# Second mixer's end: later spreads, layer norm's bias on VectorE, one root behind the tanh

## The chip, the cores and the metric

The kernel runs on one core of one Trainium2 chip, in one launch. Its time is the device time of an execution in microseconds, the median of several runs. Engines: TensorE (PE: matmuls; PEld: its weight loads), VectorE (DVE), ScalarE (ACT), GpSimd (POOL), SyncE (SP, here only DMA issues). Each engine runs its own queue in order; semaphores tie them together.

## The reference, cut to what matters

Two transformer blocks on 512 tokens of width 1024, in float32: attention beside a state space mixer and a feed-forward layer, then a block whose mixer has two halves. The change touches only the end of this second mixer:

```python
y_conv = conformer_conv(u_a, u_b, ...)          # 4 chunks of 128 channels
y_ret = retention_group(hq, hk, hv, hg)         # 4 heads of 128 channels
y = concatenate([y_conv, y_ret]) @ w_out

def conformer_conv(u_a, u_b, dw_w, dw_b, ln_w, ln_b):
    y = conv(u_a * sigmoid(u_b), dw_w) + dw_b   # depthwise, 31 taps
    return silu(layernorm(y, ln_w, ln_b))       # over 512 channels

def retention_group(hq, hk, hv, hg):
    q, k = rotary(hq), rotary(hk)               # per head
    o = chunkwise_retention(q, k, hv)
    o = o * rsqrt(mean(o * o) + EPS)            # per head and token
    return silu(hg) * o
```

## The kernel before

Everything lies with channels on the 128 partitions and the 512 tokens along the free axis. A matrix product in float32 is made of three reduced-precision matmuls (`exact`, L497 to L499): high weights by high input, high by low, low by high. So each weight unit (128 output channels by 1024 input channels, 8 tiles) is split by ScalarE into its high half (`split`, L1123) and by GpSimd into its low half, in a ring of four slots; and each input chunk must be there as a high half (a copy on ScalarE) and a low half (a subtraction on VectorE).

The second mixer first makes its inputs by units: a and b for the convolution, then q2, k2, v2, g2 for each of four heads (`unit2`, 24 matmuls each). Beside them VectorE works off the list of convolution taps (`taps`, L2628), each of which reads the accumulator that the previous tap of its channel chunk wrote. For each head: the rotation of query and key (`rotate`, and for the last head `rotated_last`, L2644), the scores (`ret_scores`, L946), `decayed`, the values (`ret_values`, L964), the square on ScalarE (`ret_square`, L1714), its column sums on TensorE (`ret_sum`, L972), the root on ScalarE (`row_root`, L1719), the reciprocal root on VectorE (`ret_var` L2669, `row_factor` L2673 to L2679), its spread over all partitions on TensorE (`spread`, L980), and `ret_norm` on VectorE (L2688, L2690), whose result ScalarE copies (`ret_high`, L1723). Sqrt and Tanh are in different tables of ScalarE: `load_root_table` is a tiny Sqrt that brings the first one in (L1160).

The convolution ends with `conv_out` on ScalarE (L1678), the mean over channels on TensorE (`conv_mean`, L990), `centre` on VectorE (L2698), squares on ScalarE (L1771), their sums (`conv_squares`, L1000), the root, the factor and a spread as above. Then for each of four chunks: `ln_scale` (VectorE, L2703), `ln_tanh` (ScalarE: a tanh, L1781, and an affine copy, L1783), `conv_silu` (VectorE, L2708), `conv_high` (ScalarE, L1787) and `conv_rest` (VectorE, L2713), which releases the chunk to TensorE.

TensorE's first three outputs of out2 are made chunk by chunk of the input (`out2_chunk`, 9 matmuls each), in the order of `OUT2_CHUNKS` = (4, 5, 6, 0, 1, 2, 3, 7): heads one to three, the four convolution chunks, the fourth head. Among these calls stand the last steps of the fourth head. The other outputs follow without a wait for inputs. The order on each engine is written out by hand, and it alone decides what waits for what.

Of the kernel before, what the change touches and what calls it, by code (L numbers as in the profile page):

```python
# [9 lines left out]
ALU = mybir.AluOpType  # L10
# [167 lines left out]
def block_program(nc, weights, x, p, vectors, constants, att_tables, ret_tables, acs_dram, out):  # L178
# [3 lines left out]
    def place(name, shape, dt=F32, at=None):  # L182

        size = 4 * int(np.prod(shape[1:]))
        offset = top[0] if at is None else at
        if at is None:
            top[0] += (size + 31) // 32 * 32
        return nc.alloc_sbuf_tensor_at(name, shape, dt, offset=offset)
# [81 lines left out]
    r_v = place("r_v", [P, T], at=r_at + 4 * K)  # L270
    r_g = place("r_g", [P, 2, T], at=r_at + 6 * K)
    ln_t = place("ln_t", [P, 4, T], at=work)
    rot_q = place("rot_q", [P, T], at=t_at)
    rot_k = place("rot_k", [P, T], at=t_at + 2 * K)
    rot_s = place("rot_s", [P, 2, T], at=t_at + 4 * K)
# [39 lines left out]
    def sem(name):  # L315
        if name not in sems:
            sems[name] = nc.alloc_semaphore(name)
        return sems[name]
# [44 lines left out]
    with block:  # L363
# [126 lines left out]
        def _(pe):  # L490
# [437 lines left out]
            def unit2(name, between={}, apart=0, bank=None):  # L928

                job = JOBS[name]  # L930
                pe.wait_ge(lo_done, job.unit + 1)
                pe.wait_ge(out_free[job.bank], job.m + 1 - apart)
                for t in range(TILES):
                    if t in between:
                        between[t]()
                    last = exact(ps[job.bank if bank is None else bank][:], job.unit % RING, t, u_hi[:, t, :], u_lo[:, t, :],
                                 t == 0, t == TILES - 1, job.unit)
                last.then_inc(out_ready[job.bank], 1)
# [44 lines left out]
            def ret_spread(h):  # L983
                spread(6, ROW["ret", h]).then_inc(sem("ret_rb"), 1)

            def conv_mean(c0, c1):

                for c in range(c0, c1):
                    pe.wait_ge(sem("conv_done"), max(c + 1, 3))
                    last = mm(ps[2][:], ones, cv[:, c, :], start=(c == 0), stop=(c == 3))  # L990
                if c1 == 4:
                    last.then_inc(sem("mean_sum"), 1)
# [12 lines left out]
            def out2_chunk(n):  # L1005

                c = OUT2_CHUNKS[n]
                if c >= 4:
                    pe.wait_ge(sem("ret_split"), c - 3)
                else:  # L1010
                    pe.wait_ge(sem("conv_split"), c + 1)
                for j in range(3):
                    job = JOBS["out2", j]
                    if n == 0:
                        pe.wait_ge(lo_done, job.unit + 1)
                        if job.bank < 2:
                            pe.wait_ge(out_free[job.bank], job.m + 1)
                        else:
                            pe.wait_ge(sem("conv_done"), 4)
                    last = exact(ps[job.bank][:], job.unit % RING, c, v_hi[:, c, :], v_lo[:, c, :], n == 0, n == C8 - 1)  # L1020
                    if n == C8 - 1:
                        last.then_inc(out_ready[job.bank], 1)
# [7 lines left out]
            for h in range(R_HEADS):  # L1030
# [9 lines left out]
                    ret_sum(h - 1)  # L1040
                if h < last_head:
                    unit2(("g2", h))
            unit2(("g2", last_head), {3: lambda: ret_spread(last_head - 1), 5: lambda: conv_mean(0, 3)})
            conv_mean(3, 4)
            ret_scores(last_head)
            values_turn(last_head)
# [4 lines left out]
            spread(2, ROW["ln"]).then_inc(sem("ln_rb"), 1)  # L1051
            ret_sum(last_head)
            out2_chunk(1)
            out2_chunk(2)
            ret_spread(last_head)
            for n in range(3, C8):
                out2_chunk(n)
            for c in range(3, WHOLE):
                job = JOBS["out2", c]
                pe.wait_ge(lo_done, job.unit + 1)  # L1060
                if job.bank < 2:
                    pe.wait_ge(out_free[job.bank], job.m + 1)
                for t in range(TILES):
                    last = exact(ps[job.bank][:], job.unit % RING, t, v_hi[:, t, :], v_lo[:, t, :], t == 0, t == TILES - 1)
                last.then_inc(out_ready[job.bank], 1)
# [48 lines left out]
        def _(act):  # L1114
# [593 lines left out]
            def ret_square(h):  # L1708
                act.wait_ge(sem("retained"), h + 1)
                if h:  # L1710
                    act.wait_ge(sem("ret_summed"), h)
                else:
                    act.wait_ge(sq_used, STATS["pre2"][0])
                af(sq[:, 0, :], ps[7][:], ACT.Square).then_inc(sem("ret_squared"), 1)  # L1714

            def row_root(n):
                act.wait_ge(sem("row_var"), n + 1)
                var, sd, _ = ROW_AT[n]
                af(tiny[:, sd:sd + QB], tiny[:, var:var + QB], ACT.Sqrt).then_inc(sem("row_sd"), 1)  # L1719

            def ret_high(h):
                act.wait_ge(sem("ret_normed"), h + 1)
                af(v_hi[:, h + 4, :], r_o[:], ACT.Copy).then_inc(sem("ret_hi"), 1)  # L1723
# [49 lines left out]
            gate_tanh(last_head)  # L1773
            load_root_table()
            row_root(ROW["ln"])
            ret_square(last_head)
            row_root(ROW["ret", last_head])

            def ln_tanh(c):
                act.wait_ge(sem("ln_scaled"), c + 1)  # L1780
                af(ln_t[:, c, :], cv[:, c, :], ACT.Tanh, scale=0.5, bias=half[:, c:c + 1]).then_inc(sem("ln_tanh"), 1)  # L1781
                act.wait_ge(sem("ln_tanh"), c + 1)
                af(cv[:, c, :], cv[:, c, :], ACT.Identity, scale=0.5, bias=half[:, c:c + 1]).then_inc(sem("ln_biased"), 1)  # L1783

            def conv_high(c):
                act.wait_ge(sem("conv_silu"), c + 1)
# [2 lines left out]
            ln_tanh(0)  # L1789
            ln_tanh(1)  # L1790
            conv_high(0)
            ret_high(last_head)
            ln_tanh(2)
            conv_high(1)
            ln_tanh(3)
            conv_high(2)
            conv_high(3)

            q, _ = STATS["post2"]
            for c in range(WHOLE):  # L1800
# [136 lines left out]
        def _(dve):  # L1937
# [763 lines left out]
            def ln_scale(c):  # L2701
                dve.wait_ge(sem("ln_rb"), 1)
                stt(out=cv[:, c, :], in0=cv[:, c, :], scalar=v("ln_w", c), in1=ps[2][:], op0=ALU.mult, op1=ALU.mult)\  # L2703
                    .then_inc(sem("ln_scaled"), 1)

            def conv_silu(c):
                dve.wait_ge(sem("ln_biased"), c + 1)
                stt(out=cv[:, c, :], in0=ln_t[:, c, :], scalar=1.0, in1=cv[:, c, :], op0=ALU.add, op1=ALU.mult)\  # L2708
                    .then_inc(sem("conv_silu"), 1)

            def conv_rest(c):
# [39 lines left out]
            ret_var(2)  # L2751
            taps(115, 117)
            row_factor(ROW["ret", 2])
            taps(117, 119)
            ret_norm(2)
            taps(119, len(CONV_TAPS))
            rotate(3)
            rotated_last()
            for c in range(4):
# [5 lines left out]
            row_var(ROW["ln"], ps[2][:, 0:QB], D_CONV)  # L2765
            row_factor(ROW["ln"])
            ln_scale(0)
            ln_scale(1)
            ret_var(3)
            ln_scale(2)  # L2770
            ln_scale(3)
            row_factor(ROW["ret", 3])
            conv_silu(0)
            ret_norm(3)
            conv_rest(0)
            conv_silu(1)
            conv_rest(1)
            ret_rest(3)
            conv_silu(2)
            conv_rest(2)  # L2780
            conv_silu(3)
            conv_rest(3)


            halved_norm("post2", y_u, "fpre2", 40)
# [291 lines left out]
```

## Time and profile before

| what | us |
| --- | --- |
| median of 3 runs | 1786.79 |
| lowest and highest of them | 1786.18 to 1786.8 |
| the profiled execution's own time | 1786.4 |
| its span in the trace | 1784.6 |
| TensorE busy | 1753.3 |
| VectorE busy | 842.1 |
| ScalarE busy | 767.9 |
| GpSimd busy | 783.8 |

The span is what the trace covers; the execution's own time has 1.8 us around it. Busy times of the engines overlap. TensorE's granted clock was full in this stretch. The end of a matmul is modelled, so matmuls that follow each other directly overlap in the rows. Times inside the trace are counted from the span's start.

### The profile page before, as it was taken

The numbers are of one execution on the slowest core, as the hardware profiler recorded it, in microseconds if no ns is written. First come the engines' busy times: TensorE is split into PE (matmuls) and PEld (weight loads), VectorE is DVE, ScalarE is ACT, GpSimd is POOL, SyncE is SP. The second block draws the span as 40 slices with busy tenths as digits, with TensorE's granted clock in tenths as the row PEclk, the third lists the DMA queues.
The fourth block names the chain that finished last, engine by engine and source line by source line (L and its number), as shares of the span: only waits on it lengthen the run. The fifth ranks groups of instructions, "written<-read, shape, count | busy, mean of one in ns | idle before, by whom it ended". The sixth has DMA issues, their size and how long they took to land.

```text
span 1784.6 us, 24772 instructions
## 1 busy us (share of the span) xinstructions
PE 1753.3 (98%) x8990; PEld 1452.4 (81%) x8990; DVE 842.1 (47%) x1587; ACT 767.9 (43%) x1269; POOL 783.8 (44%) x603
## 2 busy tenths in 40 slices
PE   7999999999999999999999999999999999999998
PEld 5777788888888888888888888988779888888877
DVE  7654546677777311263111113799847433320044
ACT  6444654566664322443222234445565323222253
POOL 3322344433343555515444446265442544445543
PEclk9999999999999999999999999999999999999998
DMA  5222233332323223314222323132221332233321
GB/s 200 72 63 81 72 108 112 112 107 95 107 95 130 95 94 96 117 49 153 94 96 94 96 95 116 61 106 71 71 79 52 107 100 99 94 95 106 106 83 48
DMA packets 47950, 170.70 MB, mean 96 GB/s; under 512 B 5457, under 2 KB 7633, under 8 KB 47601
## 3 DMA queue, kind: packets, MB, share of 16 engines
q1 hardware_dynamic: 44496, 156.25, 26.9%
q10 hardware_dynamic: 3360, 13.17, 2.2%
q8 instruction: 62, 1.02, 0.2%
q14 instruction: 32, 0.25, 0.0%
HBM read 167.24 MB, written 2.16 MB: 95 GB/s over the span
## 4 chain that ended last, share of the span: by engine, by line
PE 95%; DVE 3%; ACT 1%; issue 0%; DMA 0%; DVEq 0%; POOLq 0%; POOL 0%; SPq 0%; ACTq 0%
PE bank L497 29%; PE bank L499 28%; PE bank L498 28%; DVE bank L2628 1%; PE bank L707 1%; PE bank L855 1%; PE bank L716 1%; PE bank L729 1%; PE bank L859 1%; PE bank L839 1%; PE bank L535 1%; PE bank L830 0%; PE bank L964 0%; PE bank L946 0%; PE bank L613 0%
## 5 line engine op out<-in xcount | busy, mean ns | idle before, releaser
L411 POOL TENSOR_TENSOR w_lo<-raw,w_hi 128x512 fp32r<-128x512 f32 x472 | 619.3, 1334 | 783.9 <-ACT w_hi L1123 783.9
L497 PE MATMUL bank<-u_hi,w_hi 128*128 128x512 f32 (+1 forms) x1456 | 567.3, 390 | 3.6 <-DVE tmp L2547 3.4
L499 PE MATMUL bank<-u_hi,w_lo 128*128 128x512 f32 (+1 forms) x1456 | 557.9, 383 | 0.0
L498 PE MATMUL bank<-u_lo,w_hi 128*128 128x512 f32 (+1 forms) x1456 | 557.1, 383 | 0.0
L1123 ACT ACTIVATE w_hi<-raw 128x1024 fp32r<-128x1024 f32 x279 | 293.3, 1052 | 264.8 <-PE bank L499 262.0
L497 PEld LDWEIGHTS bank<-u_hi,w_hi 128*128 128x128 f32 x1456 | 274.1, 188 | 58.1 <-issue 7.0
L499 PEld LDWEIGHTS bank<-u_hi,w_lo 128*128 128x128 f32 x1456 | 274.0, 188 | 54.7
L498 PEld LDWEIGHTS bank<-u_lo,w_hi 128*128 128x128 f32 x1456 | 274.4, 188 | 51.3 <-issue 0.2
L419 POOL TENSOR_TENSOR w_lo<-raw,w_hi 128x512 fp32r<-128x512 f32 x84 | 111.0, 1344 | 185.7 <-ACT w_hi L1123 185.7
L497 PE MATMUL bank<-v_hi,w_hi 128*128 128x512 f32 (+1 forms) x368 | 133.8, 364 | 2.8 <-DVE v_lo L2713 2.8
L498 PE MATMUL bank<-v_lo,w_hi 128*128 128x512 f32 (+1 forms) x368 | 133.0, 361 | 0.0
L499 PE MATMUL bank<-v_hi,w_lo 128*128 128x512 f32 (+1 forms) x368 | 133.0, 361 | 0.0
L2628 DVE SCALAR_TENSOR_TENSOR bank<-cat,vec,bank 128x512 f32<-128x512 f32 x120 | 83.5, 751 | 4.3 <-ACT bank L1674 3.4
L2268 DVE SCALAR_TENSOR_TENSOR post<-bank,vec,post 128x511 f32<-128x511 f32 (+2 forms) x96 | 71.8, 748 | 27.1 <-ACT post L1304 22.0
L2547 DVE SCALAR_TENSOR_TENSOR tmp<-bank,tmp 128x512 f32<-128x512 f32 x32 | 22.1, 692 | 125.3 <-ACT tmp L1599 125.3
L497 PEld LDWEIGHTS bank<-v_hi,w_hi 128*128 128x128 f32 x368 | 69.4, 189 | 14.4 <-DVE v_lo L2713 3.8
L2559 DVE TENSOR_TENSOR ffn_acc<-ffn_acc,bank 128x512 f32<-128x512 f32 x29 | 19.9, 687 | 127.3 <-PE bank L499 127.3
L499 PEld LDWEIGHTS bank<-v_hi,w_lo 128*128 128x128 f32 x368 | 69.4, 189 | 10.7
L498 PEld LDWEIGHTS bank<-v_lo,w_hi 128*128 128x128 f32 x368 | 69.5, 189 | 10.6
L1952 DVE TENSOR_TENSOR diag<-diag,sq 128x512 f32<-128x512 f32 x24 | 21.9, 913 | 105.9 <-ACT sq L1143 105.8
L497 PE MATMUL bank<-h_hi,w_hi 128*128 128x512 f32 x176 | 68.5, 389 | 0.0
L498 PE MATMUL bank<-h_lo,w_hi 128*128 128x512 f32 x176 | 68.5, 389 | 0.0
(369 smaller groups left out, 2562.1 us busy)
## 6 DMA issues: line engine op xcount, KB each, us to landing
raw<-weights SPq DMA_DIRECT2D x289, 512.0 KB, 3.6
bc<-acs ACTq DMA_DIRECT2D x16, 512.0 KB, 3.9
xs<-x SPq DMA_DIRECT2D x4, 512.0 KB, 7.4
xs<-x ACTq DMA_DIRECT2D x1, 2048.0 KB, 7.9
rt<-ret_tables ACTq DMA_DIRECT2D x1, 1536.0 KB, 6.5
out<-xs SPq DMA_DIRECT2D x12, 128.0 KB, 1.8
dist<-att_tables SPq DMA_DIRECT2D x1, 512.0 KB, 3.3
p_raw<-p ACTq DMA_DIRECT2D x1, 512.0 KB, 7.3
```

What stands on the lines that cost most here:

```text
L411: return nc.gpsimd.tensor_tensor(w_lo[:, slot, w], raw[:, slot, w], w_hi[:, slot, w].bitcast(F32), ALU.subtract)
L419: last = nc.gpsimd.tensor_tensor(lo[:, w], raw[:, u % RING, w], hi[:, w].bitcast(F32), ALU.subtract)
L497: mm(dst, high[:, w], hi, start=first, stop=False)
L498: mm(dst, high[:, w], lo, start=False, stop=False)
L499: return mm(dst, low[:, w], hi, start=False, stop=last)
L535: last = mm(ms[:, 2 * h + t:2 * h + t + 1], part[:, t * P:(t + 1) * P], ones[:, 0:1], start=(n == 0), stop=(n == len(parts) - 1))
L1123: af(halves(u, slot)[0], raw[:, slot, :], ACT.Copy).then_inc(hi_done, 1)
L1952: tt(diag[:], diag[:], sq[:, c % 2, :], ALU.add).then_inc(sq_used, 1)
L2268: last = stt(out=post[:, now, back:T], in0=ps[job.bank][:, 0:T - back], scalar=vec[:, tap:tap + 1], in1=post[:, now, back:T], op0=ALU.mult ...
L2547: stt(out=tmp[:, j % 2, :], in0=ps[bank][:], scalar=0.0, in1=tmp[:, j % 2, :], op0=ALU.max, op1=ALU.mult).then_inc(out_free[j % 2], 1)
L2559: tt(ffn_acc[:, j, :], ffn_acc[:, j, :], ps[j % 2][:], ALU.add).then_inc(out_free[j % 2], 1)
L2628: stt(out=ps[2 + c % 2][:], in0=cat31[:, c, t:t + T], scalar=vec[:, at:at + 1], in1=ps[2 + c % 2][:], op0=ALU.mult, op1=ALU.add).then_inc( ...
```

## The change

On TensorE, `ret_spread` of the third head moves from ahead of tile 3 of the last g2 unit to ahead of tile 6, and the mean of the first three convolution chunks from tile 5 to tile 7. `ret_spread` of the fourth head moves from behind out2_chunk(2) to behind out2_chunk(5). On ScalarE, a tiny Tanh behind the layer norm's root brings the tanh table in ahead of the last square; the affine copy of `ln_tanh` goes; the last head's root moves behind the fourth tanh, with a load of the root table ahead of it and ahead of conv_high(2); `ret_high` of the last head moves to the end. On VectorE, the affine copy comes back as `ln_bias`, into a new tile `ln_b`, with a drain ahead of it and one ahead of each `conv_silu`; the last tap goes ahead of the third head's norm; and the steps of the four chunks are interleaved anew, with row_factor, conv_silu(3), ret_norm(3), conv_rest(3) and ret_rest(3) last, in this order. Nothing else is computed, and no DMA changes.

```diff
--- before.py
+++ after.py
@@ -270,6 +270,7 @@
     r_v = place("r_v", [P, T], at=r_at + 4 * K)
     r_g = place("r_g", [P, 2, T], at=r_at + 6 * K)
     ln_t = place("ln_t", [P, 4, T], at=work)
+    ln_b = place("ln_b", [P, 4, T], at=work + 17 * K)
     rot_q = place("rot_q", [P, T], at=t_at)
     rot_k = place("rot_k", [P, T], at=t_at + 2 * K)
     rot_s = place("rot_s", [P, 2, T], at=t_at + 4 * K)
@@ -1040,7 +1041,7 @@
                     ret_sum(h - 1)
                 if h < last_head:
                     unit2(("g2", h))
-            unit2(("g2", last_head), {3: lambda: ret_spread(last_head - 1), 5: lambda: conv_mean(0, 3)})
+            unit2(("g2", last_head), {6: lambda: ret_spread(last_head - 1), 7: lambda: conv_mean(0, 3)})
             conv_mean(3, 4)
             ret_scores(last_head)
             values_turn(last_head)
@@ -1051,10 +1052,11 @@
             spread(2, ROW["ln"]).then_inc(sem("ln_rb"), 1)
             ret_sum(last_head)
             out2_chunk(1)
-            out2_chunk(2)
-            ret_spread(last_head)
-            for n in range(3, C8):
+            for n in range(2, C8 - 1):
                 out2_chunk(n)
+                if n == 5:
+                    ret_spread(last_head)
+            out2_chunk(C8 - 1)
             for c in range(3, WHOLE):
                 job = JOBS["out2", c]
                 pe.wait_ge(lo_done, job.unit + 1)
@@ -1773,14 +1775,12 @@
             gate_tanh(last_head)
             load_root_table()
             row_root(ROW["ln"])
+            af(tiny[:, 60:61], tiny[:, 63:64], ACT.Tanh)
             ret_square(last_head)
-            row_root(ROW["ret", last_head])
 
             def ln_tanh(c):
                 act.wait_ge(sem("ln_scaled"), c + 1)
                 af(ln_t[:, c, :], cv[:, c, :], ACT.Tanh, scale=0.5, bias=half[:, c:c + 1]).then_inc(sem("ln_tanh"), 1)
-                act.wait_ge(sem("ln_tanh"), c + 1)
-                af(cv[:, c, :], cv[:, c, :], ACT.Identity, scale=0.5, bias=half[:, c:c + 1]).then_inc(sem("ln_biased"), 1)
 
             def conv_high(c):
                 act.wait_ge(sem("conv_silu"), c + 1)
@@ -1789,12 +1789,14 @@
             ln_tanh(0)
             ln_tanh(1)
             conv_high(0)
-            ret_high(last_head)
             ln_tanh(2)
             conv_high(1)
             ln_tanh(3)
+            load_root_table()
             conv_high(2)
+            row_root(ROW["ret", last_head])
             conv_high(3)
+            ret_high(last_head)
 
             q, _ = STATS["post2"]
             for c in range(WHOLE):
@@ -2703,9 +2705,14 @@
                 stt(out=cv[:, c, :], in0=cv[:, c, :], scalar=v("ln_w", c), in1=ps[2][:], op0=ALU.mult, op1=ALU.mult)\
                     .then_inc(sem("ln_scaled"), 1)
 
+            def ln_bias(c):
+                dve.drain()
+                ts(ln_b[:, c, :], cv[:, c, :], 0.5, half[:, c:c + 1], ALU.mult, ALU.add)
+
             def conv_silu(c):
-                dve.wait_ge(sem("ln_biased"), c + 1)
-                stt(out=cv[:, c, :], in0=ln_t[:, c, :], scalar=1.0, in1=cv[:, c, :], op0=ALU.add, op1=ALU.mult)\
+                dve.wait_ge(sem("ln_tanh"), c + 1)
+                dve.drain()
+                stt(out=cv[:, c, :], in0=ln_t[:, c, :], scalar=1.0, in1=ln_b[:, c, :], op0=ALU.add, op1=ALU.mult)\
                     .then_inc(sem("conv_silu"), 1)
 
             def conv_rest(c):
@@ -2751,9 +2758,8 @@
             ret_var(2)
             taps(115, 117)
             row_factor(ROW["ret", 2])
-            taps(117, 119)
+            taps(117, len(CONV_TAPS))
             ret_norm(2)
-            taps(119, len(CONV_TAPS))
             rotate(3)
             rotated_last()
             for c in range(4):
@@ -2765,21 +2771,25 @@
             row_var(ROW["ln"], ps[2][:, 0:QB], D_CONV)
             row_factor(ROW["ln"])
             ln_scale(0)
+            ln_bias(0)
             ln_scale(1)
+            conv_silu(0)
+            ln_bias(1)
             ret_var(3)
             ln_scale(2)
-            ln_scale(3)
-            row_factor(ROW["ret", 3])
-            conv_silu(0)
-            ret_norm(3)
             conv_rest(0)
             conv_silu(1)
+            ln_bias(2)
+            ln_scale(3)
             conv_rest(1)
+            conv_silu(2)
+            ln_bias(3)
+            conv_rest(2)
+            row_factor(ROW["ret", 3])
+            conv_silu(3)
+            ret_norm(3)
+            conv_rest(3)
             ret_rest(3)
-            conv_silu(2)
-            conv_rest(2)
-            conv_silu(3)
-            conv_rest(3)
 
 
             halved_norm("post2", y_u, "fpre2", 40)
```

## Rows read from the trace of the kernel before

**Rows 1.** The page: span, and section 1 (busy us, share of span, instructions).
```profile
span 1784.6 us, 24772 instructions
...
PE 1753.3 (98%) x8990; PEld 1452.4 (81%) x8990; DVE 842.1 (47%) x1587; ACT 767.9 (43%) x1269; POOL 783.8 (44%) x603
```

**Rows 2.** TensorE's waits from 1270 to 1345 us: us in total, times, longest us.
```profile
PE bank L497 <- DVE v_lo L2713: 2.8, 3, 2.1
PE bank L980 <- DVE tiny L2679: 1.8, 1, 1.8
PE bank L972 <- ACT sq L1714: 0.2, 1, 0.2
```

**Rows 3.** Timeline, TensorE, g2, mean, scores: start us, us, line, [idle before <-releaser].
```profile
1276.24 0.39 PE L499 MATMUL bank<-u_hi,w_lo 128*128 128x512 f32 x1
1278.42 0.65 PE L980 MATMUL bank<-cst,tiny 128*128 128x128 f32 x4 [1.79 <-DVE tiny L2679]
...
1284.94 1.02 PE L990 MATMUL bank<-cv,cst 128*128 128x512 f32 x2
1285.80 2.32 PE L946 MATMUL bank<-rot_q,rot_k 128*128 128x512 f32 x8
```

**Rows 4.** Timeline, VectorE, the same stretch.
```profile
1278.28 1.54 DVE L2628 SCALAR_TENSOR_TENSOR bank<-cat,vec,bank 128x512 f32<-128x512 f32 x2
...
1283.67 0.68 DVE L2644 TENSOR_TENSOR rot_k<-rot_k,rot_s 128x512 f32<-128x512 f32 x1
1285.99 2.49 DVE L2698 SCALAR_TENSOR_TENSOR cv<-bank,cv 128x512 f32<-128x512 f32 x4 [1.64 <-PE bank L990]
```

**Rows 5.** Timeline, ScalarE, the same stretch: ret_high(2), then conv_out(3).
```profile
1281.21 0.63 ACT L1723 ACTIVATE v_hi<-r_o 128x512 fp32r<-128x512 f32 x1 [4.33 <-DVE r_o L2690]
1281.88 0.69 ACT L1678 ACTIVATE cv<-bank,vec 128x512 f32<-128x512 f32 x1
```

**Rows 6.** Timeline, TensorE, from the last spread to the last chunk.
```profile
1302.37 0.60 PE L980 MATMUL bank<-cst,tiny 128*128 128x128 f32 x4
1305.12 0.50 PE L497 MATMUL bank<-v_hi,w_hi 128*128 128x512 f32 x1 [2.15 <-DVE v_lo L2713]
...
1310.39 0.50 PE L497 MATMUL bank<-v_hi,w_hi 128*128 128x512 f32 x1 [0.26 <-DVE v_lo L2713]
...
1312.58 0.39 PE L497 MATMUL bank<-v_hi,w_hi 128*128 128x512 f32 x1
...
1314.65 0.39 PE L497 MATMUL bank<-v_hi,w_hi 128*128 128x512 f32 x1
```

**Rows 7.** Timeline, VectorE: ln_scale, row_factor's ends, ret_norm.
```profile
1297.06 1.41 DVE L2703 SCALAR_TENSOR_TENSOR cv<-cv,vec,bank 128x512 f32<-128x512 f32 x2 [1.37 <-PE bank L980]
...
1299.76 0.17 DVE L2673 RECIPROCAL tiny<-tiny 128x4 f32<-128x4 f32 x1
...
1300.50 0.17 DVE L2679 SCALAR_TENSOR_TENSOR tiny<-tiny 128x4 f32<-128x4 f32 x1
...
1303.01 0.69 DVE L2688 SCALAR_TENSOR_TENSOR r_g<-r_g,bank 128x512 f32<-128x512 f32 x1 [0.71 <-PE bank L980]
1303.77 0.69 DVE L2690 TENSOR_TENSOR r_o<-r_g,bank 128x512 f32<-128x512 f32 x1
```

**Rows 8.** Timeline, ScalarE: the last square, the load, the first tanh.
```profile
1296.62 0.60 ACT L1714 ACTIVATE sq<-bank 128x512 f32<-128x512 f32 x1 [1.86 <-PE bank L964]
...
1298.79 1.28 ACT L1781 ACT_TABLE_LOAD   x1
1300.09 0.72 ACT L1781 ACTIVATE ln_t<-cv,half 128x512 f32<-128x512 f32 x1
```

**Rows 9.** Tensor-by-scalar L2186: source view (min/median/max ns), then one of the timeline.
```profile
L2186 DVE TENSOR_SCALAR logits<-logits,tiny x48: 286/420/1525, 37.1 to 203.6; 128x128 f32<-128x128 f32 x12, 128x256 f32<-128x256 f32 x12, 128x384 f32<-128x384 f32 x12, 128x512 f32<-128x512 f32 x12
...
202.93 0.49 DVE L2186 TENSOR_SCALAR logits<-logits,tiny 128x512 f32<-128x512 f32 x1
```

**Rows 10.** Timeline, GpSimd, up to the first weights behind the stretch.
```profile
1316.72 11.44 POOL L419 TENSOR_TENSOR w_lo<-raw,w_hi 128x512 fp32r<-128x512 f32 x8 [27.94 <-ACT w_hi L1123]
```

## The prediction

> **What bounds the kernel now.** First the page's busy times: TensorE is busy 98% of the span [rows 1]. So an edit of the other engines can only win back gaps of TensorE, and the change adds and removes no matmul. Next the waits of TensorE in the stretch from 1270 to 1345 us, the end of the second mixer [rows 2]. They are all that the change can remove there: 1.8 us behind the third head's factor, 0.2 us behind a square and 2.8 us in three waits for the low half of a convolution chunk (v_lo, L2713). That is 4.8 us of 1786.8, or 0.27%. To it comes a little for each restart: the printed idle time runs from the modelled end of a matmul, 0.39 us after its start, though an unbroken follower starts 0.23 us after it (the nine matmuls of a chunk take 2.07 us, 1312.58 to 1314.65, and after a wait 2.19 us, 1310.39 to 1312.58) [rows 3, 6]. So one full wait costs its idle time plus 0.16 + 0.12 = 0.28 us.
>
> Last the three timelines side by side, TensorE, VectorE and ScalarE, for the two places where it stands still. Those are worked through now; times are trace times of the profiled execution, whose span is 1784.6 us [rows 1], while its own time was 1786.4 us and the median of three runs is 1786.79 us. Everything behind the stretch is released by TensorE, or by an engine that waits for TensorE, so I carry a shift of the last out2 matmul to the end in full.
>
> **Part one: the third head's spread, later.** Before, TensorE computes three tiles of g2, then stands 1.79 us until 1278.42 for the factor that VectorE ends at about 1278.4 [rows 3]. After, it has six tiles first: 9 more matmuls by 0.23 us from 1276.47, which is 1278.5. The factor is there, the wait is gone with 0.1 us to spare, and all that follows could start 1.95 us earlier (2.18 us from the last matmul to the spread less the usual 0.23). The scores, at 1285.80 before, would start at 1283.85.
>
> What is late next: the scores need the rotated query and key, and those are VectorE's. VectorE has no idle time from 1278.28 to 1284.35 (0.68 us from 1283.67) [rows 4]. The edit only swaps the last tap of the convolution ahead of the norm of head three. It makes that tap wait for its predecessor (two chained taps take 1.54 us, 0.77 each, where an operation that waits for nothing holds VectorE 0.60, four in 2.49 [rows 4]), so I put the rotated sums 0.1 us later, at about 1284.45. The scores then start at 1284.5, not at 1283.85: 1.3 us earlier, less 0.1 for the restart. On the way, conv_out(3) on ScalarE stands behind ret_high(2), which waits for the norm. Before, it ended at 1281.88 + 0.69 = 1282.57 [rows 5]; now the norm ends 0.75 later, at about 1281.95, then 0.63 and 0.69 us less their overlap give 1283.2. TensorE wants it at 1284.94 - 1.95 = 1283.0 [rows 3], so there is a wait of 0.3 us, but it lies ahead of the one for the rotation and costs nothing of its own. The centring (1.64 us idle before it [rows 4]) can move up by about 1.6 us, more than TensorE. So everything up to ret_values, the spread of ln and ln_scale moves by **1.2 us**; bounds 1.0 (both waits cost a restart) and 1.6 (VectorE as quick as before and the means no obstacle).
>
> **Part two: the end, counted from ln_scale(0)'s start, S** (1297.06 before [rows 7], about 1295.9 after). In front of S, the tanh table: ScalarE is idle 1.86 us in front of the last square [rows 8]. A load takes 1.28 us and its tiny activation some 0.2, 1.5 in all, so it is hidden with 0.35 us to spare. If it weren't, the square and the sum would be late by the excess, one for one. ret_sum's own 0.25 us wait stays.
>
> Durations on VectorE: 0.69 to 0.70 us for a 512-column operation on two tensors (0.60 to the next start when nothing is awaited), and 0.76 from start to start over a drain (1303.01 to 1303.77 [rows 7]). The new ln_bias is a 128x512 tensor-by-scalar operation between two SBUF tiles. The nearest row is one of 0.49 us; the same line goes up to 1.53 us elsewhere, though its median is 0.42 [rows 9]. Here GpSimd is idle 27.94 us up to 1316.72 [rows 10], so I take 0.49; 0.69, the duration of the two-tensor forms, is the bound within this stretch, 1.53 the far one.
>
> The new VectorE order then runs: ln_scale(0) to S+0.7, bias 1.26, ln_scale(1) 1.9, silu(0) 2.65, bias 3.2, ln_scale(2) 3.9, rest(0) 4.55, silu(1) 5.3, bias 5.9, ln_scale(3) 6.5, rest(1) 7.15, silu(2) 7.9. ScalarE fits between: tanh 0.72, copy 0.63 [rows 5, 8], each begun 0.04 us after its input. TensorE has no spread in its way now and wants chunk 0 at S+5.31 (1302.37 before [rows 6]), chunk 1 at 7.37 and chunk 2 at 9.43. The first two are ready at 4.6 and 7.2: both waits go.
>
> Chunk 2 isn't. ScalarE ends the last tanh at 7.25, loads the root table and runs its tiny activation to 8.65, and only then copies: 9.28. rest(2) ends at 10.0, chunk 2 starts at 10.07 and ends at 12.26. The root (0.2 us beside this) and VectorE's row factor (0.91 us, 1299.76 to 1300.67 [rows 7]) are done at 10.85, so the spread starts at 12.26 with no wait.
>
> **Then the old long wait returns at a new place.** On VectorE conv_rest(3) stands behind ret_norm(3), which waits for this spread. Before, conv_rest(0) stood there. From the spread's start (1302.37) over the two norms and the low half to the next chunk (1305.12) it took 2.75 us, of which TensorE was idle 2.15 [rows 6, 7]. After, it is the same four steps in front of chunk 3: 12.26 + 2.75 = 15.01. Chunk 3 ends at 17.20, chunk 7 (fourth head, whose copy and low half are done by 15.8) at 19.27. Before, that point was 1314.65 + 2.07 - 1297.06 = 19.66. Part two gives **0.4 us**: the 0.6 us that the three waits of L497 hold beside the long one [rows 2], and the two restarts, are won, chunk 2's wait of about 0.5 and its restart are new, and the 2.15 stays. Bounds: -0.4 with ln_bias at 0.69 (three of them ahead of rest(1) and rest(2), 0.6 us, and another restart), +0.9 if chunk 2's wait doesn't show.
>
> **Sum.** 1.2 + 0.4 = 1.6 us off 1786.79: **1785.2 us**. By the bounds 0.6 to 2.5 us off, 1784.3 to 1786.2. About 0.2%, 3.6 us, is what a measurement of this kernel tells from no change; this is less.
>
> **The table load, by row and by rule.** The load in front of the first tanh starts at 1298.79 and the tanh follows at 1300.09, so a switch costs 1.30 us here and nothing unseen [rows 8]. The Trainium skill, ScalarE: Activation LUTs, section What ACT_TABLE_LOAD costs, puts some 1.38 us of drain on top of it, about 2.66 us for a switch. That speaks against a load put between the last tanh and the third copy; the row speaks against the rule. It is rival C.
>
> **The rivals.**
> A, all gaps go. If chunk 3's low half did not hang on the spread, 4.8 us and four restarts would go, 0.2 us less for the square's wait: some 5.3 us off, 1781.5. For it: the waits are this large. Against: the order in the diff, conv_rest(3) behind ret_norm(3), and that exactly this order costs 2.15 us now. Chance 0.04.
> B, the front does nothing. If the rotation or the fourth channel's mean comes later than worked out (the margin of the spread is 0.1 us), part one is only a wait moved from the spread to the scores; part two alone leaves 1786.4. For it: VectorE has no slack there at all. Against: TensorE's 1.64 us of delay to the centring is real slack. Chance 0.09.
> C, the load costs more behind real work. As a mechanism: another 1.38 us between the last tanh and conv_high(2), with nothing in front of chunk 2 to absorb it, so chunk 2, the spread and chunk 3 are all late by it: 1785.2 + 1.4 = 1786.6. For it: no load of before is timed between dependent copies. Against: the 1.30 us. Chance 0.07.
> D, slower: ln_bias becomes VectorE's bound. At 1.53 us each, the three ahead of rest(1) and rest(2) add 3 x 1.04 = 3.1 us, and chunks 1 and 2 wait: 1788.3. It turns to a loss once one costs 1.6 / 3 = 0.53 us more than 0.49, that is above 1.02 us. For it: the 1.53 us of the same line, if they come from two engines at the same memory at once. Against: GpSimd has no work in the stretch [rows 10]. Chance 0.04.
>
> **How the numbers follow.** Forecast 0.72, A 0.04, B 0.09, C 0.07, D 0.04, and 0.04 for what I don't see. The range takes in the forecast's bounds, B and C, with a few tenths for the spread of the runs (1786.18 to 1786.8): 1784.1 to 1786.9. Faster by over 0.2% needs 3.6 us: A and a little, 0.05. Slower by as much: more than D, 0.02. Within: 0.93.
>
> **What would show it.** TensorE's waits in this stretch: none in front of L980 in g2; one of about 0.1 to 0.4 us in front of the scores (L946), released by the rotated sums of VectorE; none in front of chunks 0 and 1; about 0.5 us in front of chunk 2 and about 2.1 us in front of chunk 3, right behind the last spread. Each ln_bias 0.49 us. A tanh table load inside the idle time in front of the last square. Wrong, if the long wait is missing (A), if L946 waits 1.5 us (B), if the first copy behind the last load starts over 2 us after the load did (C), or if ln_bias takes over 1 us (D).

## The result and the profile after

The changed kernel takes 1788.91 us, the median of 20 runs from 1787.40 to 1791.73; the kernel before took 1786.70 us beside it (20 runs, 1785.84 to 1787.05). The ratio is 1.0015 with a 95% interval from 1.0009 to 1.0021: slower, by 2.2 us from median to median and by 2.6 us from mean to mean, and the interval does not reach 1. I had forecast 1785.2 us, from 1784.1 to 1786.9, so the time lies outside the range and on the other side.

The page of the profiled execution (1788.93 us, span 1787.1 us), to be set beside [rows 1]:

```profile
span 1787.1 us, 24782 instructions
...
PE 1754.4 (98%) x8990; PEld 1453.0 (81%) x8990; DVE 847.8 (47%) x1591; ACT 765.6 (43%) x1267; POOL 783.3 (44%) x603
```

TensorE's waits from 1270 to 1345 us, as in [rows 2] (us in total, times, longest):

```profile
PE bank L498 <- DVE v_lo L2720: 2.7, 2, 2.1
PE bank L947 <- DVE rot_k L2646: 1.9, 1, 1.9
PE bank L973 <- ACT sq L1716: 0.2, 1, 0.2
PE bank L991 <- ACT cv L1680: 0.2, 1, 0.2
```

The wait for the factor (1.8 us) is gone, and one of 1.9 us for the rotated sums stands in its place; I had forecast 0.1 to 0.4 us. The sum of the waits, 5.0 us, is hardly above the 4.8 of before. So waits alone don't explain the loss. The timelines of VectorE and GpSimd in that stretch, where [rows 4] has 0.68 us for the second sum:

```profile
1278.47 2.33 DVE L2630 SCALAR_TENSOR_TENSOR bank<-cat,vec,bank 128x512 f32<-128x512 f32 x3
...
1281.47 0.69 DVE L2692 TENSOR_TENSOR r_o<-r_g,bank 128x512 f32<-128x512 f32 x1
...
1283.39 1.33 DVE L2646 TENSOR_TENSOR rot_q<-rot_q,rot_s 128x512 f32<-128x512 f32 x1
1284.65 1.74 DVE L2646 TENSOR_TENSOR rot_k<-rot_k,rot_s 128x512 f32<-128x512 f32 x1
```

```profile
1282.90 1.28 POOL L453 TENSOR_TENSOR v_lo<-r_o,v_hi 128x512 fp32r<-128x512 f32 x1 [4.85 <-ACT v_hi L1725]
1284.43 3.10 POOL L420 TENSOR_TENSOR w_lo<-raw,w_hi 128x512 fp32r<-128x512 f32 x2 [0.25 <-ACT w_hi L1125]
```

Each sum is under way while GpSimd subtracts: the first ends 0.54 us after GpSimd's low half of head three (1284.18), the second under GpSimd's next pair. In the kernel before, both sums (1283.06 to 1284.35) ran where GpSimd was idle, but for the first 0.13 us:

```profile
1281.75 1.28 DVE L2637 TENSOR_TENSOR rot_s<-bank,rt 128x512 f32<-128x512 f32 x2
1283.06 0.69 DVE L2644 TENSOR_TENSOR rot_q<-rot_q,rot_s 128x512 f32<-128x512 f32 x1
```

```profile
1281.91 1.28 POOL L452 TENSOR_TENSOR v_lo<-r_o,v_hi 128x512 fp32r<-128x512 f32 x1 [4.05 <-ACT v_hi L1723]
1286.27 2.51 POOL L419 TENSOR_TENSOR w_lo<-raw,w_hi 128x512 fp32r<-128x512 f32 x2 [3.07 <-ACT w_hi L1123]
```

And TensorE's own rows, beside [rows 3]:

```profile
1283.46 1.12 PE L991 MATMUL bank<-cv,cst 128*128 128x512 f32 x2 [0.22 <-ACT cv L1680]
1286.45 4.11 PE L947 MATMUL bank<-rot_q,rot_k 128*128 128x512 f32 x8 [1.86 <-DVE rot_k L2646]
1290.40 0.60 PE L956 MATMUL bank<-cst,r_v 128*128 128x128 f32 x4
```

The scores, the same eight matmuls, take 4.11 us instead of 2.32. The view by windows (length, then busy time and instructions of PE, PEld, DVE, ACT, POOL, then the granted clock, DMA share, GB/s) says why:

```profile
1284.00:1286.00 2.00, 0.58 (x2) 0.00 (x0) 2.00 (x2) 0.35 (x1) 1.75 (x3) 1.00 0.00 0
1286.00:1288.00 2.00, 1.55 (x2) 0.64 (x3) 2.00 (x4) 0.97 (x2) 1.52 (x1) 0.70 0.00 0
1288.00:1290.00 2.00, 2.00 (x6) 1.39 (x5) 2.00 (x5) 1.45 (x3) 0.00 (x0) 0.50 0.65 199
```

Behind the wait the granted clock is 0.50, the 1.2 GHz level, until about 1290. In the trace of before it was full all through the stretch, at the scores too:

```profile
1288.00:1290.00 2.00, 2.00 (x18) 1.78 (x17) 2.00 (x4) 1.98 (x4) 0.78 (x1) 1.00 0.02 2
```

Last, far behind the change, a wait of TensorE that before did not have, and VectorE's row ahead of it:

```profile
1388.13 0.69 DVE L2826 TENSOR_TENSOR sq<-sq,bank 128x512 f32<-128x512 f32 x1
1389.24 1.76 DVE L2806 SCALAR_TENSOR_TENSOR h_tmp<-sq,h_scale 128x512 f32<-128x512 f32 x1 [0.42 <-issue]
```

```profile
1396.93 0.50 PE L498 MATMUL bank<-u_hi,w_hi 128*128 128x512 f32 x1 [0.67 <-DVE sq L2834]
```

The same product in the kernel before, where nothing stood in front of it, and TensorE's same matmul, which did not wait:

```profile
1386.87 0.86 DVE L2796 SCALAR_TENSOR_TENSOR h_tmp<-sq,h_scale 128x512 f32<-128x512 f32 x1
```

```profile
1394.08 0.40 PE L497 MATMUL bank<-u_hi,w_hi 128*128 128x512 f32 x1
```

"Issue" is idle time for which the profile shows no releaser. So there are three suspects: GpSimd beside the rotated sums, the clock behind the wait, and the gap in VectorE's stream.

**Where the time lies.** The first 1270 us shift by up to 2.7 us from one execution to the next (over all traces here), so I count from an anchor, the start of the third head's column sums (1273.53 before, 1273.68 after), and take the rest from the start of the fourth out2 unit (which is where the last chunk ends, 1316.69 before and 1318.71 after) to the end of the span.

| us | before | after |
| --- | --- | --- |
| scores start | 12.27 | 12.77 |
| values_turn starts | 14.42 | 16.72 |
| fourth out2 unit starts | 43.16 | 45.03 |
| from there to the end | 467.91 | 468.39 |

The stretch costs 1.87 us, all of it ahead of values_turn (2.30), and 0.43 us come back behind it. The rest costs 0.5, in two steps. Counted matmul by matmul from the fourth unit on, both traces keep the same distances until the wait at 1396.93 (1394.08 before); behind it the changed kernel is 0.93 us later, and stays so until about 1770. Then some 0.4 us come back, where the granted clock of the two executions differs (1775 to 1780 us, before and after):

```profile
1775.00:1780.00 5.00, 2.23 (x5) 0.81 (x4) 4.44 (x15) 0.00 (x0) 2.34 (x3) 0.50 0.25 83
1775.00:1780.00 5.00, 4.11 (x22) 2.81 (x22) 3.12 (x12) 1.88 (x3) 1.23 (x2) 0.83 0.31 103
```

### The profile page after: what moved, and what is told of

The parts are those of the page before. It is cut to its first block, busy times and chain, and to the rows that moved or that the text cites. A ratio compares the mean times of both kernels' runs of the same rounds, so it can differ in the third digit from the quotient of the medians.

```text
span 1787.1 us, 24782 instructions
## 1 busy us (share of the span) xinstructions
PE 1754.4 (98%) x8990; PEld 1453.0 (81%) x8990; DVE 847.8 (47%) x1591; ACT 765.6 (43%) x1267; POOL 783.3 (44%) x603
## 4 chain that ended last, share of the span: by engine, by line
PE 93%; DVE 5%; ACT 1%; issue 1%; DMA 0%; DVEq 0%; POOLq 0%; POOL 0%; SPq 0%; ACTq 0%
PE bank L498 28%; PE bank L500 28%; PE bank L499 28%; DVE bank L2630 1%; PE bank L708 1%; PE bank L856 1%; PE bank L717 1%; PE bank L730 1%; PE bank L860 1%; PE bank L840 1%; PE bank L536 1%; PE bank L831 0%; PE bank L947 0%; PE bank L965 0%; PE bank L818 0%
```

## The experiments

e1 to e4 ran on one chip and the others on another, each group beside the kernel before, whose median was 1786.48 us with e1 to e4, 1786.53 with e5 to e8 and 1786.44 with e9 to e12; so e2 can be set against e5 to e8 to within a tenth. Medians are of 11 runs; the last three columns are of one profiled execution of each, counted as above: the start of the scores and of the fourth unit from the anchor, and the rest. Beside the kernel before, only e1 and e3 (slower) and e12 (faster) are clear of their 95% intervals, which are some 0.1% (1.6 us) wide to either side; where another kernel's median is set against before, the trace has to carry the argument.

| kernel | median (lowest to highest) | scores | fourth unit | rest |
| --- | --- | --- | --- | --- |
| e1_front_only | 1788.62 (1787.06 to 1789.11) | 12.75 | 45.54 | 467.56 |
| e2_back_only | 1787.79 (1786.59 to 1788.38) | 12.27 | 42.97 | 468.49 |
| e3_kept_clock | 1788.44 (1787.57 to 1789.07) | 12.75 | 43.29 | 468.75 |
| e4_late_split | 1786.42 (1784.80 to 1789.06) | 11.69 | 42.24 | 469.09 |
| e5_back_kept | 1787.62 (1785.74 to 1788.55) | 12.26 | 42.96 | 468.47 |
| e6_back_padded | 1786.52 (1785.65 to 1787.45) | 12.27 | 44.61 | 467.57 |
| e7_old_taps | 1785.39 (1784.69 to 1788.48) | 10.91 | 43.02 | 469.36 |
| e8_rest_first | 1786.15 (1783.47 to 1786.85) | 12.26 | 42.10 | 468.50 |
| e9_before_padded | 1787.84 (1786.32 to 1788.69) | 12.27 | 43.18 | 468.81 |
| e10_front_old_taps | 1785.08 (1783.64 to 1785.63) | 10.92 | 42.04 | 467.52 |
| e11_old_taps_padded | 1785.70 (1781.87 to 1786.52) | 10.92 | 43.08 | 467.58 |
| e12_rest_first_padded | 1783.36 (1782.53 to 1784.79) | 10.92 | 40.62 | 467.69 |

**Each part alone.** e1_front_only is the kernel before with

```diff
-            unit2(("g2", last_head), {3: lambda: ret_spread(last_head - 1), 5: lambda: conv_mean(0, 3)})
+            unit2(("g2", last_head), {6: lambda: ret_spread(last_head - 1), 7: lambda: conv_mean(0, 3)})
...
-            taps(117, 119)
+            taps(117, len(CONV_TAPS))
             ret_norm(2)
-            taps(119, len(CONV_TAPS))
```

> Part one of the change alone: the third head's spread and the means later on TensorE, the last tap ahead of its norm on VectorE; all else as before. Theory P (two engines at one memory, then the clock): the whole loss is here. Both rotated sums of VectorE take 1.3 and 1.7 us beside GpSimd instead of 0.69, the scores wait about 1.9 us, and they then run at half the granted clock, 4.1 us instead of 2.3: 1.5 to 2.5 us slower than before, with runs that differ by more than those of before. Theory Q (the loss lies in the new end, with its table loads and its moved spread): part one alone gains the 1.2 us that I had forecast for it, about 1785.5 us.

e2_back_only is the changed kernel with these lines as they were.

> Part two of the change alone: ln_bias on VectorE, the tables' order, the fourth head's spread later; front as before. Theory P: 0.2 to 0.4 us faster than before (1786.3 to 1786.5 us), the long wait of 2.15 us still there ahead of chunk 3, the rotated sums 0.69 us each, the clock full at the scores, runs as close together as those of before. Theory Q: 1.5 to 3 us slower than before.

e1 is 2.1 us slower than before, with sums of 1.34 and 1.74 us, the wait of 1.9 us and slow scores (values_turn at 16.55): theory P holds for part one, and Q falls. But e2 missed both forecasts. Its stretch gains 0.19 us as P says (42.97 against 43.16), its sums take 0.69 us, and yet its median is 1.3 us above before. Its last column is longer, 468.49 against 467.91, with the issue gap and the 0.7 us wait of the changed kernel in its trace (0.95 us at that wait, part of it won back in the last 15 us); e1 has neither. That is not all of the 1.3 us: the profiled execution is e2's fastest, 1786.59 us, and what its other runs lose beyond it no kept trace shows.

**The clock.** e3 puts matmuls of constants into the wait:

```diff
             conv_mean(3, 4)
+            evicted(("v2", last_head))
+            keep_clock(2, bank=0)
             ret_scores(last_head)
```

> The changed kernel with two matmuls of constants (512 columns, into a free bank) in the wait ahead of the last scores, so that TensorE isn't idle there; the rotated sums stay slow. Theory C (the scores are slow only because the granted clock fell after the wait): the scores take 2.3 us again and the time falls by about 1.8 us against the changed kernel, to about 1787.1 us. Rival M (the scores are slow because rotated query and key are being written or read by others at that time): the scores still take about 4.1 us, the time stays at 1788.9 us.

```profile
1284.88 1.88 PE L614 MATMUL bank<-cst 128*128 128x512 f32 x4
1286.91 2.42 PE L947 MATMUL bank<-rot_q,rot_k 128*128 128x512 f32 x8 [0.16 <-DVE rot_k L2648]
```

The scores take 2.42 us again at a full granted clock, though they start as late as in the changed kernel and though its two sums are as slow (1.33 and 1.75 us). So their length was the clock's, and rival M falls. Its stretch is 1.74 us shorter than the changed kernel's (43.29 against 45.03), as forecast. The median fell by 0.5 us only. In the profiled pair 0.8 us go against the gain outside the stretch: the anchor is 0.48 us later (1274.16 against 1273.68) and the rest 0.36 us longer, though both have the gap. Whether the same holds for the other runs isn't shown.

**GpSimd.** e4 leaves TensorE alone and moves ScalarE's next high half, and with it GpSimd's next subtraction, behind the squares:

```diff
             conv_out(3)
-            refill(("g2", last_head))
             for c in range(4):
                 act.wait_ge(sem("centred"), c + 1)
                 af(ln_t[:, c, :], cv[:, c, :], ACT.Square).then_inc(sem("centred_squared"), 1)
+            refill(("g2", last_head))
```

> The changed kernel with ScalarE's high half of the next weight unit behind the four squares, so that GpSimd's two subtractions for it come behind the rotated sums and not beside them; GpSimd's low half of head three still meets the first sum. Theory P: the sum for the key takes 0.69 us instead of 1.74, the one for the query stays at about 1.3; the scores start 1.0 us earlier, their wait is about 0.8 us, and the clock stays full behind so short a wait: 1.0 + 1.8 = 2.8 us off the changed kernel, 1786.1 us (1787.9 if the clock falls all the same). Rival: if the sums are slow for another reason than GpSimd, nothing changes, 1788.9 us.

```profile
1282.67 1.33 DVE L2646 TENSOR_TENSOR rot_q<-rot_q,rot_s 128x512 f32<-128x512 f32 x1
1283.93 0.68 DVE L2646 TENSOR_TENSOR rot_k<-rot_k,rot_s 128x512 f32<-128x512 f32 x1
```

```profile
1282.18 1.27 POOL L453 TENSOR_TENSOR v_lo<-r_o,v_hi 128x512 fp32r<-128x512 f32 x1 [4.84 <-ACT v_hi L1725]
1288.69 2.55 POOL L420 TENSOR_TENSOR w_lo<-raw,w_hi 128x512 fp32r<-128x512 f32 x2 [5.23 <-ACT w_hi L1125]
```

Both halves of the forecast came true: the sum that no longer meets GpSimd takes 0.68 us, the one that still does 1.33. The wait is 0.80 us, the clock stays full, and the stretch is 2.79 us shorter than the changed kernel's, against 2.8 forecast. The median is 1786.42 us against 1786.1 forecast; three of the eleven runs are at 1788.3 to 1789.1. The same rows show a rule of the Trainium skill at work (SBUF — State Buffer, section Who interferes with whom): a VectorE instruction with two inputs in SBUF contends with a GpSimd instruction that reads SBUF, and one with at most one SBUF input, outside the modes that use both port pairs, does not. The trace agrees on the second half too: in the kernel before, rotate(3), whose operations have one input in PSUM, took 1.28 us for two from 1281.75 on, though GpSimd's low half of head three stood beside them (1281.91 to 1283.19).

**The swapped tap.** e7 is the changed kernel with the last tap behind the norm as before; e10 is the kernel before with TensorE's line of e1 alone.

> The changed kernel with the last tap back behind the third head's norm, as before; TensorE's and ScalarE's orders as changed. Theory P: the norm is 0.75 us earlier, so GpSimd's low half of head three is over before the rotated sums or nearly so, and its next work starts later than they do: 0.7 to 0.9 us each instead of 1.33 and 1.74. The scores wait under 0.6 us, the clock stays full there, and 1.5 us of wait and 1.8 us of slow scores come back: 1785.5 to 1786.0 us. Rival (GpSimd still meets both): 1788.9 us.

> The kernel before with TensorE's part of part one alone (third head's spread at tile 6, means at tile 7); the last tap stays behind the norm. Theory P (it was the swapped tap that brought the rotated sums beside GpSimd): the sums take 0.69 us, the scores start 1.2 to 1.4 us earlier than before, and the time is 1785.2 us where the clock stays full. Rival (moving the spread alone is enough to shift GpSimd onto the sums): as e1_front_only, 1788.6 us.

e7's VectorE and TensorE:

```profile
1283.28 0.69 DVE L2646 TENSOR_TENSOR rot_q<-rot_q,rot_s 128x512 f32<-128x512 f32 x1
1283.89 0.68 DVE L2646 TENSOR_TENSOR rot_k<-rot_k,rot_s 128x512 f32<-128x512 f32 x1
```

```profile
1284.63 2.43 PE L947 MATMUL bank<-rot_q,rot_k 128*128 128x512 f32 x8 [0.50 <-DVE rot_k L2646]
```

```profile
1282.13 1.29 POOL L453 TENSOR_TENSOR v_lo<-r_o,v_hi 128x512 fp32r<-128x512 f32 x1 [4.05 <-ACT v_hi L1725]
1284.44 2.52 POOL L420 TENSOR_TENSOR w_lo<-raw,w_hi 128x512 fp32r<-128x512 f32 x2 [1.02 <-ACT w_hi L1125]
```

One line of VectorE's order makes up 3.5 us by the medians, 1785.39 against 1788.91 us. In the traces the stretch is 2.0 us shorter (43.02 against 45.03), and that with 1.6 us of slow chunks, told below, which the changed kernel's execution did not have. The norm is early enough that GpSimd's low half of head three is nearly over when the first sum begins (1283.42 against 1283.28), and the second sum is under way when the next subtraction starts. e10, at 1785.08 us, is 1.4 us under before by the medians, and its stretch is 1.1 us shorter (42.04 against 43.16): about what I had forecast for part one (1.2). The lower six of e7's runs are at 1784.7 to 1785.4 us, the other five at 1786.8 to 1788.5. The profiled one, 1787.97 us, is one of those: the clock fell behind the wait ahead of chunk 3.

```profile
1308.00:1312.00 4.00, 1.86 (x8) 1.32 (x7) 2.67 (x4) 1.25 (x2) 0.00 (x0) 0.86 0.00 0
1312.00:1316.00 4.00, 4.00 (x14) 3.21 (x13) 0.00 (x0) 0.39 (x1) 0.00 (x0) 0.72 0.00 0
```

That is the wait of 2.14 or 2.15 us that all kernels but e5, e8 and e12 have, ahead of chunk 3 in the changed order and ahead of chunk 0 in the old one. In their eleven profiles the clock fell behind it five times (e1, e6, e7, e10, e11). In the changed order it then costs 1.6 us (e6 against e2: 44.61 and 42.97). In the old one it costs 0.3 (e1 from the fourth head's column sums to the fourth unit: 19.75 us, before 19.42), because the slower chunks then only fill the two small waits that follow there.

**The long wait.** e5 fills it in part two alone (`keep_clock(2)` behind `ret_spread(last_head)`), and e8 takes its cause away:

```diff
-            ret_norm(3)
             conv_rest(3)
+            ret_norm(3)
             ret_rest(3)
```

> Part two alone (as e2_back_only) with two matmuls of constants, 512 columns each, right behind the fourth head's spread, in the long wait ahead of chunk 3. e2_back_only was profiled at 1786.6 us with a full clock at that wait, but 9 of its 11 runs took 1787.3 to 1788.4 us. Theory C (in those runs the granted clock falls behind the long wait): all runs come together near 1786.6 us, over 1 us below e2_back_only's median of 1787.79. Rival (they differ for another reason, such as the state of a DMA or of a queue): the median stays at 1787.8 us and the spread at 1.5 us.

> Part two alone with conv_rest(3) ahead of ret_norm(3) on VectorE, so that chunk 3 no longer waits for the fourth head's spread and norm. By the times of the trace chunk 3 then waits 0.5 us instead of 2.14 and the last chunk some 0.4 us: 1.4 us less than e2_back_only, 1786.4 us; and if the clock fell there because of the long wait, it no longer does, which is another 1.2 us: 1785.2 us. Rival (the long wait only moves to the fourth head's chunk): no gain, 1787.8 us.

e5 missed: the wait is down to 0.43 us in its trace, but its median stays at 1787.62 us and its runs still stand in two groups. So the clock behind this wait is not what divides the runs of e2_back_only. e8 came out at 1786.15 us, 1.6 us under e2, with waits of 0.6, 0.5 and 0.4 us; of the stretch, 0.87 us are gained, less than the 1.4 I expected: chunk 3 starts 1.6 us earlier, but chunk 7 waits 0.42 us and a restart, which I had left out.

**The gap in the stream.** e6 adds drains to e2 behind ret_rest(3), and e9 adds the same to the kernel before, behind conv_rest(3), and nothing else:

```diff
+            for _ in range(12):
+                dve.drain()
```

> Part two alone with twelve more drains on VectorE behind ret_rest(3), where it is idle for over 5 us. They do nothing but move the later instructions of VectorE by twelve places in its stream. Theory F (the longer stream puts a 0.43 us gap without a releaser in front of a product of the feed-forward part, which then meets GpSimd, takes 1.76 instead of 0.86 us and lets TensorE wait 0.7 us for a bank): the gap moves to another place, that wait is gone and 0.7 to 1.0 us come back against e2_back_only, about 1787.0 us. Rival (the gap comes from the time or from a transfer, not from the place in the stream): gap, 1.76 us and wait stay, 1787.8 us.

> The kernel before with twelve drains on VectorE where it is idle behind conv_rest(3): as many instructions as the change adds to VectorE (four ln_bias, eight drains), so that all later ones stand at the same place of the stream as in the changed kernel, and nothing else is changed. Theory F (a gap that belongs to the place in the stream): the 0.43 us gap without a releaser and the 1.76 us product appear in the feed-forward part as in the changed kernel, TensorE waits 0.7 us there, and the kernel is 0.7 to 1.0 us slower than before, 1787.4 us. Rival (the gap comes with the changed order, not with the number of instructions): as before, 1786.5 us.

In e6 the gap in front of the product and the 0.7 us wait are gone, and the median falls by 1.27 us to 1786.52. In e9 twelve instructions that do nothing, in idle time, make both appear; the median is 1.4 us above before's, and the profiled execution loses 0.95 us at that wait:

```profile
1388.14 1.75 DVE L2797 SCALAR_TENSOR_TENSOR h_tmp<-sq,h_scale 128x512 f32<-128x512 f32 x1 [0.43 <-issue]
```

```profile
PE bank L497 <- DVE sq L2825: 0.7, 1, 0.7
```

Over all traces the rest is 468.4 to 469.4 us in the eight with the gap there (after, e2 to e5, e7 to e9) and 467.5 to 467.9 us in the six without. Counted by matmuls from the fourth unit, the eight are 0.93 to 0.95 us later than before behind the wait and the other six at most 0.02; what else differs in that column lies in the last 15 us. And in all eight the product behind the gap is the 1896th instruction of VectorE that the trace holds, drains included, whichever order or time it has: it is the place that decides. What happens at that place the traces don't say.

**All of it.** e11 is e7 with the twelve drains, e12 is e11 with conv_rest(3) ahead of ret_norm(3).

> The changed kernel with the last tap back behind the norm and twelve more drains behind ret_rest(3): two of the three causes taken out. e7_old_taps had 1785.39 us; the wait of 0.7 us with its restart should go as well: 1784.5 us where the clock stays full, and runs some 1.7 us above it where it falls behind the 2.14 us wait, as e7_old_taps had them in 5 of 11.

> As e11_old_taps_padded, and conv_rest(3) ahead of ret_norm(3) on VectorE: all of the changed kernel that gains, without what loses. The stretch gains 1.4 us of the long wait on top of e11_old_taps_padded: 1783.2 us, and with no wait over 0.6 us left in it hardly a run should show a fallen clock. If the theory of the long wait is wrong, 1784.5 us as e11.

e11 missed by 1.2 us; four of its runs are at 1781.9 to 1784.5, the other seven at 1785.7 to 1786.5, and in its profile the clock fell behind the 2.15 us wait. e12 came out at 1783.36 us, 0.2 from its forecast, and in its stretch the granted clock is full. But the second half of that forecast, that hardly a run would show a fallen clock, missed: five of its eleven runs are at 1784.0 to 1784.8 us with a mean granted clock of 0.994, the other six at 1782.5 to 1783.4 with 0.997. It beats both kernels: 3.1 us under before, ratio 0.9984, interval 0.9975 to 0.9993. Its waits in the stretch:

```profile
PE bank L498 <- DVE v_lo L2720: 1.1, 2, 0.6
PE bank L947 <- DVE rot_k L2646: 0.5, 1, 0.5
PE bank L498 <- DVE v_lo L2696: 0.4, 1, 0.4
PE bank L973 <- ACT sq L1716: 0.2, 1, 0.2
```

## Why the prediction was wrong

**The step that failed** is in part one: "so I put the rotated sums 0.1 us later, at about 1284.45". I carried over 0.68 us for a sum from [rows 4] without asking who else was at work then. In the prediction I looked at GpSimd only for the second part [rows 10]. Its work in the first part hangs on two things that the change itself moves, the third head's high half (0.8 us later from the anchor, by the swapped tap) and the high half of the next weight unit (2.0 us earlier, because TensorE ends g2 earlier). Together they closed the gap in which the sums had run. The sums ended at 1286.39, 1.9 us later than I said, with 0.15 us of it from the anchor. e4 and e7 show it, and e10, with the sums at 0.69 and 0.68 us, shows that the rest of part one held.

**The price of a wait.** I counted the wait that took the place of the old one by its idle time and a restart. Behind 1.86 us of it the scores ran at half the clock and cost 1.8 us more. Nothing in the trace of before showed such a price, since its clock was full behind waits of 1.79 and 2.15 us; I should have kept it as a bound of its own, as it is worth more than any gain in the sum. e3 shows it. Rival B had the place right (the scores wait in the spread's stead), and its sign, a wait of 1.5 us at L946, came (1.86), but it priced it at no gain, without the slower sums and without the clock. The range went no further up than B and C; a loss of this size I had only under D, for another cause.

**What twelve more instructions do elsewhere.** "Everything behind the stretch is released by TensorE ... so I carry a shift ... to the end in full" was wrong by 0.9 us at one wait in the profile, of which 0.4 came back at the end, and by 1.4 us between the medians of before and e9, for a cause that no step considered.

**What was right.** The spread at tile 6 had no wait. The steps of part two came out nearly to the tenth, counted from ln_scale(0) at 1299.28:

```profile
1309.58 0.50 PE L498 MATMUL bank<-v_hi,w_hi 128*128 128x512 f32 x1 [0.57 <-DVE v_lo L2720]
...
1311.75 0.60 PE L981 MATMUL bank<-cst,tiny 128*128 128x128 f32 x4
1314.50 0.50 PE L498 MATMUL bank<-v_hi,w_hi 128*128 128x512 f32 x1 [2.14 <-DVE v_lo L2720]
```

Chunk 2 started at 10.30 (forecast 10.07), the spread at 12.47 (12.26), chunk 3 at 15.22 (15.01), the end of the last chunk at 19.43 (19.27). Part two gave 0.2 us instead of 0.4. The return of the long wait ahead of chunk 3, against rival A, is there. ln_bias took 0.49 us in each of four, so rival D falls by its own test, though its mechanism, GpSimd beside VectorE, was the one that decided, on other instructions. The tables cost what the row said, 1.3 us, and not the 2.66 us of the Trainium skill (ScalarE: Activation LUTs, section What ACT_TABLE_LOAD costs), so rival C falls too:

```profile
1306.04 0.72 ACT L1783 ACTIVATE ln_t<-cv,half 128x512 f32<-128x512 f32 x1 [0.60 <-DVE cv L2705]
1306.78 1.28 ACT L1162 ACT_TABLE_LOAD   x1
1308.07 0.20 ACT L1162 ACTIVATE tiny<-tiny 128x1 f32<-128x1 f32 x1
1308.18 0.62 ACT L1787 ACTIVATE v_hi<-cv 128x512 fp32r<-128x512 f32 x1
```

The copy starts 1.40 us after the load does, behind a real tanh and with a tiny activation in between. Rival A's sum was 0.4 us short by its own prices: 4.6 us and four restarts of 0.28 make 5.7, not 5.3; nothing hangs on it.

**The account**, in the profiled execution: forecast -1.6 in the stretch; slower sums and their wait +1.7 (scores at 12.77 against 11.1, that is 1284.5 less the anchor, and the restart), slow scores +1.8, the end 0.2 less than forecast, which makes +2.1 where 1.87 was measured; then +0.9 at the gap's wait, -0.4 in the last 15 us and 0.15 ahead of the anchor.

**What stays open.** Runs of the same kernel stand in groups 1 to 2 us apart (e2, e5, e7, e9, e11, e12), and four of the changed kernel's twenty are at 1791.2 to 1791.7 us. The mean granted clock of the runs goes with it in most: 0.997 in the lower group of e5, e9, e11 and e12, 0.996 or less in the upper; 0.992 to 0.994 in those four, 0.994 or 0.995 in the other sixteen. So the clock goes with the groups; whether it makes them is not shown, and by e5 it is not the long wait that divides those of e2. The profiles suggest other places. From 1760 to 1780 us the granted clock is 0.82 in e12's, 0.87 in before's and full in e5's. From 40 to 50 us it is 0.66 in e9's, 0.83 in before's and full in e6's, and over these 10 us TensorE's matmuls slip 1.3 us against before's in e9 and gain 0.6 us in e6; that is part of the shift ahead of the anchor. None of this was tested. Why the clock falls behind a 2.14 us wait in some executions only is open as well.

## What to carry to other kernels

When an edit moves work on one engine, list what the others do at the new time, above all GpSimd beside VectorE instructions with both inputs in SBUF, and check which of them the edit moves too. Price a new wait of TensorE of about 2 us with the chance of a fallen clock, 1.8 us for 2.3 us of matmuls here, and not with its idle time alone. Before a small loss is put down to an order, try the old order with as many idle instructions added: here twelve of them cost 0.95 us in the trace and 1.4 us between medians.

## What was not expected of the hardware

- A sum of two SBUF tiles on VectorE (128x512) takes 0.69 us alone and 1.33 to 1.75 us where GpSimd subtracts at the same time; 0.13 or 0.14 us of overlap, at its start or its end, did not lengthen it (before, e7).
- The granted clock fell to 0.50 behind 1.86 us without matmuls, and in five of eleven profiles behind 2.14 us.
- A gap of 0.43 us without a releaser belongs to a place in VectorE's stream: twelve drains earlier in the stream make it appear or vanish in front of the same instruction, and in all eight traces that have it there, that is the 1896th that the trace holds.
